# A hybrid decoder step on 8 cores: the posts and loads of the first input projections in a new order, and 17 normed blocks turned by a DMA transpose in place of TensorE

## The reference, cut to what matters

```python
def _layer(x, prev_pool, prev_conv, prev_ffn, start_pos, ...):
    h = _rmsnorm(x, norm_mix)
    proj = h @ w_in                                      # (B,T,POOL_W+3*CONV_W)
    u  = proj[..., :POOL_W];  gb = proj[..., POOL_W:POOL_W + CONV_W]
    gc = proj[..., POOL_W + CONV_W:POOL_W + 2 * CONV_W];  v = proj[..., POOL_W + 2 * CONV_W:]
    d, new_pool = _multi_scale_pool(u, prev_pool, start_pos)   # trailing means over 2/4/8/16, minus the token
    a = jnp.einsum('btgc,gcd->btgd', d, w_pool).reshape(Bn, T, POOL_W) * pool_scale
    conv, new_conv = _causal_dwconv(gc * v, prev_conv, conv_w) # 3 taps
    b = gb * conv
    x = x + jnp.concatenate([a, b], axis=-1) @ w_out
    h = _rmsnorm(x, norm_ffn)
    up = h @ w_up                                        # (B,T,2*D_FF), D_FF = 2816
    upc, new_ffn = _causal_dwconv(up, prev_ffn, ffn_conv_w); upc = upc + ffn_conv_b
    val, gate = upc[..., :D_FF], upc[..., D_FF:]
    x = x + (jax.nn.silu(gate) * val) @ w_down
    return x, new_pool, new_conv, new_ffn
```

## Time and profile before

| | |
|---|---|
| median of 3 runs | 728.96 us (727.8 to 747.03) |
| profiled execution, its own time | 728.0 us |
| span of its slowest core (3), from first to last instruction | 726.4 us |
| spans of the 8 cores | 720.1 to 726.4 us |
| granted TensorE clock, mean by core | 0.977 to 0.985 |
| PE busy | 689.3 us (95%) |
| DVE busy | 492.2 us (68%) |
| ACT busy | 347.0 us (48%) |
| POOL busy | 215.5 us (30%) |

### The profile page before, as it was taken

The page is one execution under the profiler, slowest core; times in us unless marked ns, Lnnn a source line. Parts: engine busy times, 40 slices in busy tenths (PEclk is TensorE's granted clock), DMA queues, the critical chain, the costliest instruction groups (busy, mean ns, idle before and its releaser), DMA issues.

```text
span 726.4 us, 12730 instructions; the slowest of 8 cores (720.1 to 726.4 us)
## 1 busy us (share of the span) xinstructions
PE 689.3 (95%) x3788; PEld 334.7 (46%) x3788; DVE 492.2 (68%) x846; ACT 347.0 (48%) x809; POOL 215.5 (30%) x414
## 2 busy tenths in 40 slices
PE   5869799889999999999999999999999999999996
PEld 4534345445554454444444444444444444444442
DVE  4277767578886245788878566877777276888724
ACT  4344342567775112877643233766621234666521
POOL 2242100467774000455431000444420001443300
PEclk8989899989999999999999999999999999999999
DMA  8998593887787456999989430999987212980002
GB/s 198 234 170 125 97 214 62 131 146 132 126 137 152 67 164 166 172 189 187 184 150 164 145 117 1 177 166 163 155 144 123 105 71 54 162 135 1 4 29 88
DMA packets 26742, 94.62 MB, mean 130 GB/s; under 512 B 3358, under 2 KB 3742, under 8 KB 26674
## 3 DMA queue, kind: packets, MB, share of 16 engines
q0 software_dynamic: 18288, 66.59, 56.5%
q1 hardware_dynamic: 8242, 26.95, 11.1%
q10 hardware_dynamic: 144, 0.26, 0.1%
HBM read 150.36 MB, written 10.01 MB: 221 GB/s over the span
## 4 chain that ended last, share of the span: by engine, by line
PE 82%; DMA 7%; DVE 5%; issue 2%; ACT 2%; DVEq 0%; SPq 0%; ACTq 0%; POOL 0%; POOLq 0%
PE G L598 53%; PE G L905 12%; PE G L906 12%; DMA wslot<-w_str 3%; DMA yp<-x1b 3%; PE TR L598 2%; PE TR L554 2%; PE G L1142 1%; DMA x1b<-xp 1%; DVE w_down_sb L769 1%; DVE arena L769 1%; ACT hbuf L496 0%; DVE arena L830 0%; DVE arena L842 0%; DVE actT L558 0%
## 5 line engine op out<-in xcount | busy, mean ns | idle before, releaser
L969 ACT ACTIVATE arena<-G,cst_sb 128x512 f32<-128x512 f32 x176 | 135.4, 776 | 86.2 <-PE G L598 85.1
L598 PE MATMUL G<-aT,wslot 128*128 128x512 bf16 x736 | 165.8, 383 | 1.3 <-DVE arena L1007 1.0
L998 DVE SCALAR_TENSOR_TENSOR arena<-G,cst_sb,arena 128x512 f32<-128x512 f32 x176 | 124.0, 747 | 43.7 <-ACT Esave L974 41.0
L598 PE MATMUL G<-aT,sm_arena 128*128 128x512 bf16 x672 | 146.8, 379 | 0.0
L1007 DVE SCALAR_TENSOR_TENSOR arena<-G,cst_sb,arena 128x512 f32<-128x512 f32 x176 | 125.5, 744 | 4.9 <-DVE OFp L1005 0.5
L905 PE MATMUL G<-w_down_sb,actT 128*128 128x512 bf16 x330 | 125.1, 379 | 0.0
L906 PE MATMUL G<-w_down_sb,actT 128*128 128x512 bf16 x330 | 125.1, 379 | 0.0
L978 POOL TENSOR_TENSOR actT<-arena 128x512 bf16<-128x512 f32 x88 | 95.5, 1086 | 72.9 <-ACT arena L976 60.9
L598 PEld LDWEIGHTS G<-aT,wslot 128*128 128x128 bf16 x736 | 71.3, 99 | 85.3 <-issue 4.9
L598 PEld LDWEIGHTS G<-aT,sm_arena 128*128 128x128 bf16 x672 | 65.7, 98 | 78.6
L496 ACT ACTIVATE hbuf<-x1b 128x1024 bf16<-128x1024 f32 x29 | 30.7, 1057 | 136.5 <-DVE x1b L868 110.8
(11 more groups left out here) (167 smaller groups left out, 775.2 us busy)
## 6 DMA issues: line engine op xcount, KB each, us to landing
wslot<-w_str POOLq DMA_DIRECT2D x58, 512.0 KB, 7.3
sm_arena<-w_str POOLq DMA_DIRECT2D x50, 512.0 KB, 7.4
x1b<-xp SPq DMA_DIRECT2D x13, 512.0 KB, 5.0
yp<-x1b SPq DMA_DIRECT2D x12, 512.0 KB, 3.9
w_down_sb<-w_down POOLq DMA_DIRECT2D x11, 512.0 KB, 10.3
xrot<-xp SPq DMA_DIRECT2D x10, 512.0 KB, 6.3
w_down_sb<-w_str POOLq DMA_DIRECT2D x4, 512.0 KB, 18.9
w_out_sb<-w_out POOLq DMA_DIRECT2D x4, 512.0 KB, 15.0
```

Source lines behind the costliest of these rows:

```text
L598: ins = e.matmul(out_ap, lhsT=wslot[slot][:, k, half * 128:(half + 1) * 128], rhs=rhsT[:, k, c0:c0 + ncols], start=(k == 0), stop=(k == nk ...
L969: P.op("act", lambda e, tp=tp, g=g, c=c, h=h: e.activation(out=tp[:, h, 2:514], in_=G[g][:, :], func=AF.Identity, scale=cc(C_FW + 3 * c), ...
L998: P.op("dve", lambda e, g=g, c=c, h=h: e.scalar_tensor_tensor(out=tp[:, h, 1:513], in0=G[g][:, :], scalar=cc(C_FW + 3 * c + 1), in1=tp[:, ...
```

## The change

Two groups of edits, made together.

**Posts and loads.** (1) In `small_cv` and `main_cv` the second and third taps are held back and recorded after the pair's flush; the small first tap and the copy of the decode state move from DVE to ACT. (2) The small projections of pairs 2 and 3 go to a `G` bank in place of `TR` (`SmallBank`). (3) `w_down` pieces q = 7 to 10 (resident 11 to 14) are issued one by one behind weight pieces 13, 15, 17 and 19, which are loaded during the third stage of tile 0, in place of all four in a row ahead of it. (4) `keep_busy`, dummy matmuls of 128 columns, grows from 8 to 24, and two more stand before the first projection (10 and 16). (5) The u sums of j = 2 are flushed one pair earlier. The second norm of tile 0 scales on ACT in place of DVE.

**Turns.** `norm_transpose` gets `dma=True`: in place of `turn` two steps, a `dma_start_transpose` of `hbuf` (128 x 1024 bf16) on SyncE's queue (SP), and `weigh`, a DVE multiplication in place by the norm's weight. It is used for the n1 norms of tiles 2 and 3 (8 blocks) and for the second norm of tiles 1, 2 and 3 for i = 0 to 2 (9 blocks). The windows are written anew around it (`s2_tail`, `n1_two`, `n1_weigh`).

```diff
-        RES_AFTER = {4: (0, 1), 5: (2, 3), 7: (4,)}
+        RES_AFTER = {4: (0, 1), 5: (2, 3), 7: (4,), 13: (11,), 15: (12,), 17: (13,), 19: (14,)}
-        LATE = list(range(9, 15))
+        LATE = [9, 10]
...
+            def turn_dma():
+                P.op("sp", lambda e: e.dma_start_transpose(out=dstT[:, :, col0:col0 + 128], in_=hb[:, :]), reads=[hk],
+                     writes=dstkeys, dsem=f"D_turn{HKI[hk]}")
+
+            def weigh():
+                dst = dstT[:, :, col0:col0 + 128]
+                P.op("dve", lambda e: e.tensor_tensor(
+                    out=dst, in0=dst, in1=cst_sb[:, gcol:gcol + 8].unsqueeze(2).to_broadcast([128, 8, 128]), op=ALU.mult),
+                    reads=["cst"], writes=dstkeys)
+                hfree.append(HKI[hk])
+            if dma:
+                return Steps(scale, turn_dma, weigh)
...
-                gsm = self.smalls(slot) if small else None
+                gsm = self.smalls(slot, pi in (2, 3)) if small else None
...
                     elif kind == "v":
-                        rest = small_cv(j, gsm, half) if small else None
-                        main_cv(s, j, g, bs)
-                        if rest is not None:
-                            rest()
+                        late_s = small_cv(j, gsm, half) if small else (lambda: None)
+                        late_m = main_cv(s, j, g, bs)
+                        late += [late_s, late_m]
...
                 self.flush(pi)
+                for fn in late:
+                    fn()
...
-            return norm_transpose(x1[r], 128, [("x1", r)], hb, hk, aT, i * 128, C_G2, [("aT", k, i) for k in range(8)])
+            return norm_transpose(x1[r], 128, [("x1", r)], hb, hk, aT, i * 128, C_G2, [("aT", k, i) for k in range(8)],
+                                  act_scale=(s == 0), dma=(s >= 1 and i < 3))
...
+        def s2_tail(s, n2):
+            for i in range(len(n2), 4):
                 n2.append(s2_block(s + 1, i))
-                if i == 0:
-                    pb.pop(0)()
-                if i >= 1:
+                if i >= 2 and n2[i - 2].fns:
+                    n2[i - 2].step()
+                if i >= 1 and n2[i - 1].fns:
                     n2[i - 1].step()
-                if i >= 2:
-                    n2[i - 2].step()
+                    n2[i - 1].step()
...
-        keep_busy(8)
+        keep_busy(24)
...
-        for r in LATE[2:]:
-            load_res(r)
...
-            for fn, dj in ((n1_start, 0), (n1_scale, 2), (n1_turn, 4)):
+            for fn, dj in ((n1_start, 0), (n1_scale, 2), (n1_turn, 3), (n1_turn, 6)):
```

More of the change, by code:

```diff
@@ L650, in pair @@
                     release(slot)
+                late = []
                 for half, (kind, j) in sorted(enumerate(pair), key=lambda t: POST_RANK[t[1][0], "v" in (pair[0][0], pair[1][0])]):
@@ L691, in stage1, with subT @@
                 st.pair(next_weights(), True)
-        def subT(i, half):
-            return TRF[i][:, half * NSM:(half + 1) * NSM]
+        def subT(h, half):
+            return h.ap[:, half * NSM:(half + 1) * NSM]
         def small_u(j, gsm, half):
@@ L819, in rest @@
                      reads=[("XcvN", b), ("Tcs", b)], writes=[("Tcs", b)])
-            return rest
+            return taps
         def main_cv(s, j, g_v, bs):
@@ L1218, in window, with n1_two, n1_weigh @@
             return lambda: s4_post(s, 3, gab)()
+        def window(s):
+            nx2 = s + 2 if s + 2 < NST else None
+            pb = []
+            def n1_two(i):
+                if nx2 is None:
+                    return
+                for n in (i, i + 1):
+                    pb.append(norm1_block(nx2, n))
+                for n in (i, i + 1):
+                    pb[n].step()
+                for n in (i, i + 1):
+                    pb[n].step()
+            def n1_weigh(i):
+                for p in pb[i:i + 2]:
+                    p.step()
+            n1_two(0)
+            if nx2 is not None:
+                load_xrot(nx2, 2)
+                load_xrot(nx2, 3)
+            load_x1(s + 1, 0)
+            for i in range(3):
+                s4_block(s, i)()()
+                load_x1(s + 1, i + 1)
+                if i == 1:
+                    n1_weigh(0)
+                    n1_two(2)
+            n1_weigh(2)
+            return s2_tail(s, [])
         def window0():
@@ L1228, in window0 @@
                 if i == 0:
+                    n2[0].step()
                     n2[0].step()
@@ L1240, in window0 @@
             pump()
[L1241 to L1246 removed]
+            post3 = s2_tail(0, n2)
             load_xrot(2, 0)
             load_xrot(2, 1)
[L1249 to L1256 removed]
+            return post3
         def sample_state_outputs_s1():
```

128 lines of the change are left out of this document (51 added, 77 removed).

## The result

The changed kernel takes 752.7 us (median of 5 runs, 752.4 to 778.5). Against the kernel before it is slower by a ratio of 1.035, 95% interval 1.033 to 1.037; in some executions of either kernel the cores of a die run at a lower clock, and the ratio leaves these out. The forecast was 713, the range 705 to 728. The profiled execution took 752.4 us; its slowest core is core 7, with a span of 750.8 us, and the eight spans run from 736.6 to 750.8, wider than before.

A forecast was written before the change was run, and what follows sets the result against it. PE work was taken to bound the kernel from 150 us on, with DVE the chain from 28 to 96 us. Gains 1.0 + 6.0 + 5.5 + 3.5 = 16.0 off 728.0, plus 1.0 for the median, gave 713.0; range 705 to 728.

The forecast's parts named there:

- Part D, the hook: Third stage of tile 1: four turns leave PE and gain 1.8 us, their landing covered by three pairs, 10 us.
- L: Time from the end of `scale` on DVE to the start of `weigh`; taken as 3.0 us, ends 2.0 and 10.6.
- third rival: Slower kernel: each turn takes 5 us or more, the price paid in the s2 tails; chance 0.15.
- Part D, the windows: Turns off PE in the windows, at 3.0 us landing: window(1) gains 0.4, last tail ends as before, window0 gains 1.2.
- The sign that the prediction named: Start of third stages of tiles 2 and 3: PE waits 0 to 2 us for `weigh` or the last `TR` block.
- The 10.5 us estimated there for eight blocks: DMA turn of eight 128 x 128 blocks in a row, estimated from the skill's 1309 ns for one.
- Three times over in a row: s2 tails: each `weigh` stands in DVE's queue ahead of the next `scale`, so the landing time is paid three times.
- 1 to 2 for each microsecond: window0: gain of 1.2 us at a 3.0 us landing, then 1 to 2 us lost per further microsecond.
- Part C: Residents q = 7 to 10 moved into tile 0's third stage: sixth pair starts 6.2 us earlier, less 0.7, gain 5.5 us.
- the 3 us too much fit into the lead of four slots: Tile 0's third stage: twelve pieces take 36 us where eight pairs last 33; a 12 us lead absorbs the excess.
- Parts A and B: A: dummy matmuls before the first projection hold the clock, 1.0 us; B: reordered stage 1 posts shorten DVE's chain, 6.0 us.
- second rival: First part gains half: PE waits for `G` banks or pieces instead of DVE's bank release; 719.5 us, chance 0.15.

The follow-up runs named there:

- e5: Changed kernel with tile 2's four weighings moved to pairs 18 to 21 of tile 1's third stage, buffers given back at the turn; 778.4 us, ratio 1.066.
- e6: Changed kernel with tile 2's four norms begun at pairs 9, 11, 13, 15 of tile 1's third stage, not 2, 4, 9, 11; 770.5 us, one execution.
- e15: Kernel put together from the gaining edits (722.1 us), plus one tile 2 block turned by DMA in tile 1's third stage, weighed 14 pairs later; 729.4 us.
- e7: Changed kernel with tile 2's four turns on PE, and plain DMAs of 1024 pieces of 256 bytes issued in their place; 745.3 us, one execution.
- e10: Changed kernel with tile 2's turns on PE, and in s2 tails each block scaled and sent before the previous one is weighed; 727.6 us, ratio 0.998.
- e1: Changed kernel with tile 2's four turns, in tile 1's third stage, given back to PE, the other 13 by DMA; 738.8 us, ratio to before 1.011.
- e8: Changed kernel with tile 2's four turns on PE, and plain DMAs of 128 rows of 2 KB issued in their place; 738.2 us, one execution.
- e4: Kernel before with only w_down pieces q = 7 to 10 moved behind weight pieces 13, 15, 17 and 19; 731.2 us, ratio 1.0019.
- e13: Kernel put together from the gaining edits (722.1 us), with one w_down piece, q = 10, moved behind weight piece 19; 721.5 us, ratio 0.989.
- e14: Kernel put together from the gaining edits (722.1 us), with w_down pieces q = 9 and 10 moved behind weight pieces 17 and 19; 722.9 us, ratio 0.991.

## Why the prediction was wrong

**Part D, the hook: the step that failed.** It read: "The eight n1 blocks have cover: three pairs in the hook (3 x 3.45 = 10 us)". The longest landing there is 22 to 43 us by core, not 3. I used L = 3.0 for the hook without asking what L is beside the stream, although a row for that stood in my list: 10.64 us for a plain store under the refill. I had put its risk, and the third rival, in the s2 tails, and took the stretches for those alone; the trace of before shows a DMA share of 1.0 in every 10 us from 295 to 365 us (168 to 201 GB/s), and that is where four of the 17 turns lie. Forecast -1.8, measured +17.0 on the mean core and +26.9 on the slowest. By e5, e6 and e15 more cover at another place in that stage does not help: beside the stream the turn lands late wherever it is issued, and the x load behind it on SP lands later still. e7 shows that small pieces are enough for both; what the transposing adds on some cores stays open.

**Part D, the windows: right in mechanism, a little low in size.** L was taken as 3.0 and is 3.1 to 3.4. The sign that the prediction named came too: at the start of the third stages of tiles 2 and 3 PE waited 2.7 us in all for the last block out of `TR`, 1.3 at the longest. The 10.5 us estimated there for eight blocks did not come: 2.7 to 3.2 in those tails. "Three times over in a row" is confirmed by e10, where the order alone gives back all of it. Forecast for window(1), last tail and window0: -0.4, 0 and -1.2; measured +0.5, +0.6 and +0.3. In window0 the turns land in 2.7 to 6.9 us beside the refill (e1), which I had as "1 to 2 for each microsecond" and did not put in. The third rival had the right sign at the wrong place. What the Trainium skill's "Advanced Engine Details and Errata", X-Bar Transpose, states (as fast as a plain DMA) is not far from the quiet rows, 2.8 us against 2.0 for a plain store of the same size; beside the stream it does not hold here, 24 us and more against 13.7 for e8's plain rows of 2 KB.

**Part C: wrong in sign.** Forecast -5.5, measured +3.6 (e4: +4.1). The wait at the fifth pair goes on some cores, as said (143.84 for 149.62), but on half of the cores of before it was hardly there: core 3, which I read, had 3.7 us, cores 0 and 6 only 0.7 and 1.0, and their third stage took 93.5 where core 3's took 99. So 5.5 was what a slow core could gain, not the kernel; and in e4 not even the slow cores gained (98.1 to 100.9 on all eight). The step that failed is "the 3 us too much fit into the lead of four slots": the lead is nil there, and the four pieces left a stretch in which the DMA engines are otherwise idle (e4, e13, e14).

**Parts A and B: half the gain, lost again.** A worked: the first 32 matmuls take 2.8 us on five cores and 3.3 on the mean, for 4.7 before. B's gaps closed as listed: the taps' idle time fell from 4.6 and 2.2 us to 0.6 and 1.1. But from the first projection to s2 of tile 0 only 3.7 us are gained, of 7.0. The rest is the second rival's: 2.5 us for a weight piece at 32.66, 2.65 at 60.41 and 1.48 at 77.91 for the same small product in a new place, 3.0 for `w_out` at 92.46, which had been 0.7 on core 3. Of the 3.7, 2.8 are lost again ahead of the third stage: half by the scaling on ACT, which I had not costed at all, though the diff names it. PE waits for ACT there twice, 0.8 us each.

**Sum.** 713 forecast; A and B 6 short, C 9, the windows 3, the hook 19 on the mean core and 29 on the slowest. On the mean core that is 37 of the 40 us; the rest is that the slowest core now stands 6.8 us above the mean span, before 3.4.

## What to carry to other kernels

The price of a DMA has to be read from the stretch in which it will run, not from a quiet one: look up the DMA share at every place where the change puts one, since there a latency of 3 us can be 30, and what it costs is the thing queued behind its reader, and the next transfer queued behind it. Before loads are moved out of a busy-looking place, look whether the engines would stand idle there and whether the new place has time to spare. And where a result takes a round trip through another queue, issue the next one before consuming this one: two lines in another order gave back 3.6 and 2.2 us in the two tails.
